# An uneven pace of expert dot products beside two delta-net layers, and a re-ordered opening of the first stretch, in a one-core decoder kernel on Trainium2

## What is computed

```
def peer_ffn(h, wq, k1, k2, u, v):
    ...
    v1, i1 = lax.top_k(s1, PEER_TOPK)
    v2, i2 = lax.top_k(s2, PEER_TOPK)
    ...
    sc, pos = lax.top_k(cand, PEER_TOPK)
    idx = jnp.take_along_axis(cand_idx, pos, axis=-1)
    gate = jax.nn.softmax(sc, axis=-1).astype(h.dtype)
    ...
        ue = jnp.take(u, ib, axis=0)
        act = gb * jax.nn.gelu(jnp.einsum('nd,nkd->nk', tb, ue))
        ve = jnp.take(v, ib, axis=0)
        return jnp.einsum('nk,nkd->nd', act, ve)
```

## Time and profile before

| | |
|---|---|
| median of three executions | 1930.27 us (1926.15 to 1933.41) |
| the profiled execution | 1927.03 us |
| its span, first to last instruction | 1925.2 us |
| instructions | 22276 |
| PE / DVE / ACT / POOL busy | 79% / 69% / 22% / 30% of the span |
| mean granted TensorE clock | 0.874 of full speed |
| read from HBM | 700.82 MB, 365 GB/s over the span |

### The profile page before, as it was taken

How to read it: one execution, slowest core, us unless ns; L and a number is a source line. 1 busy time by engine, 2 the same in 40 slices (tenths; PEclk the granted TensorE clock), 3 DMA queues, 4 the chain that set the end, 5 groups by cost and what they waited for, 6 DMA issues and landing times.

```text
span 1925.2 us, 22276 instructions
## 1 busy us (share of the span) xinstructions
PE 1529.6 (79%) x7828; PEld 912.6 (47%) x7828; DVE 1334.0 (69%) x3962; ACT 418.5 (22%) x1139; POOL 583.4 (30%) x551
## 2 busy tenths in 40 slices
PE   6999999965656889888889687998889875555555
PEld 6644876511113656666558265766656641111111
DVE  6667646769976779585446776877845579778654
ACT  1221211000002722622211264154121210000001
POOL 0110223444442322322222322232232244444541
PEclk8999798667678989999899898999998987886887
DMA  9988499999998967987999998699699999999995
GB/s 368 360 319 308 183 402 376 411 422 421 421 421 356 421 270 273 421 317 277 393 409 417 391 398 321 223 388 373 232 385 396 421 379 403 421 421 421 422 422 227
DMA packets 100255, 703.32 MB, mean 365 GB/s; under 512 B 15264, under 2 KB 15648, under 8 KB 16560
## 3 DMA queue, kind: packets, MB, share of 16 engines
q0 software_dynamic: 78336, 570.46, 73.6%
q1 hardware_dynamic: 21808, 131.45, 17.0%
HBM read 700.82 MB, written 1.05 MB: 365 GB/s over the span
## 4 chain that ended last, share of the span: by engine, by line
PE 43%; DMA 20%; DVE 15%; issue 5%; ACT 5%; POOL 1%; SPq 0%; DVEq 0%; POOLq 0%; ACTq 0%
PE PS L1646 15%; DMA vb<-in_peer_uv,idx 8%; DMA ub<-in_peer_uv,idx 6%; PE PS L1796 3%; PE PS L1702 3%; PE PS L2013 3%; PE PS L1989 3%; DMA ring<-in_peer_uv,idx 2%; DVE vb L1147 2%; PE PS L1970 2%; DVE ub L1147 2%; PE PS L1749 2%; PE PS L1873 1%; ACT ring L1472 1%; DMA mods<-in_peer_uv,idx 1%
## 5 line engine op out<-in xcount | busy, mean ns | idle before, releaser
L1646 PE MATMUL PS<-ub,z 128*64 128x512 f32 x832 | 342.7, 762 | 128.4 <-DVE z L1113 125.0
L1646 PE MATMUL PS<-vb,z 128*64 128x512 f32 x828 | 318.4, 748 | 106.9 <-DVE z L1113 105.2
L2046 POOL DMA_INDIRECT ub<-in_peer_uv,idx x208 | 227.4, 1093 | 522.4 <-PE PS L1646 458.2
L2046 POOL DMA_INDIRECT vb<-in_peer_uv,idx x207 | 230.8, 1115 | 434.9 <-PE PS L1646 389.2
L1359 ACT ACTIVATE tanhs<-cubed 128x2 f32<-128x2 f32 x256 | 52.0, 203 | 879.0 <-DVE cubed L1102 855.5
L1646 PEld LDWEIGHTS PS<-ub,z 128*64 128x64 f32 x832 | 77.8, 162 | 279.0 <-DVE z L1113 184.4
L1646 PEld LDWEIGHTS PS<-vb,z 128*64 128x64 f32 x828 | 73.7, 160 | 262.9 <-DVE z L1113 170.4
L1147 DVE CUSTOM_DVE_ANT_0 vb<-vb,h 128x1024 f32<-128x1024 f32 x104 | 127.1, 1222 | 54.0 <-DMA vb<-in_peer_uv,idx 53.4
L1646 PE MATMUL PS<-mods,z 128*64 128x512 f32 x204 | 124.8, 743 | 36.9 <-DVE z L1113 34.5
L1147 DVE CUSTOM_DVE_ANT_0 ub<-ub,h 128x1024 f32<-128x1024 f32 x104 | 127.1, 1222 | 35.7 <-DMA ub<-in_peer_uv,idx 33.6
L1106 DVE SCALAR_TENSOR_TENSOR acts<-tanhs,gated_x 128x2 f32<-128x2 f32 x256 | 40.4, 158 | 152.4 <-ACT tanhs L1359 146.1
(11 more groups left out here) (364 smaller groups left out, 2780.2 us busy)
## 6 DMA issues: line engine op xcount, KB each, us to landing
ring<-in_gdn_qkv SPq DMA_DIRECT2D x32, 1024.0 KB
ring<-in_peer_wq SPq DMA_DIRECT2D x23, 1024.0 KB
two_slots<-in_ada_wide POOLq DMA_DIRECT2D x20, 1024.0 KB, 7.8
ring<-in_gdn_z SPq DMA_DIRECT2D x16, 1024.0 KB
ring<-in_gdn_w_out SPq DMA_DIRECT2D x16, 1024.0 KB
ring<-in_gla_w_in SPq DMA_DIRECT2D x6, 2048.0 KB, 11.0
mods<-in_ada_wide POOLq DMA_DIRECT2D x11, 1024.0 KB, 7.5
ring<-in_ada_w SPq DMA_DIRECT2D x4, 2048.0 KB, 11.9
```

What stands on the lines that cost most here:

```text
L1646: last = pe.matmul(y[64 * g:64 * g + 64, e, :], z[:, i % 4, g, :], rows[:, D + e * 512:D + (e + 1) * 512], start=False, stop=False, skip_g ...
L2046: pool.indirect_dma_start(row_buffers[b], None, uv_rows, off).then_inc(row_landed[b].sem, 16)
```

## The change

One kernel takes these changes together:

- `dot_at` for stretches 1 and 2 goes by a table `PACE` of (nominal time, dots done): 17 dots by 86, 45 by 164, 60 by 236, 88 by 314, 128 by 520. Routing stays at its dot numbers.
- `JOB_AT` spaces jobs 4 to 11 from 3.0 to 63.0 (from 2.5 to 39.5), and the eight "mod" blocks go from 52 + 8b to 85 + 27b; DVE's use of their sum moves to behind them.
- The first use of the row buffers goes in the order 0 to 3, 8, 9, 10, 4 to 7, so that the four in `vb` come last, and POOL waits for `cols_summed` ahead of dot 7; ahead of dots 4 and 5 it has waits of their own.
- On PE `turn_h` of tile 1 goes ahead of the 40 narrow matmuls.
- ACT's wait for the last state product of a core gets a due time of its own, later than it had.

```
-                return W_AT[w] + (W_AT[w + 1] - W_AT[w]) * (n + 1) / STRETCH
+            PACE = ((0.0, 0), (86.0, 17), (164.0, 45), (236.0, 60), (314.0, 88), (B, STRETCH))
...
+                if w in (0, 3):
+                    return W_AT[w] + A * (n + 1) / STRETCH
+                (at, of), (to, upto) = next((a, b) for a, b in zip(PACE, PACE[1:]) if n + 1 <= b[1])
+                return W_AT[w] + at + (to - at) * (n + 1 - of) / (upto - of)
...
-            JOB_AT = (-31.0, -27.0, -15.0, -11.0, 2.5, 6.5, 10.5, 14.5, 18.5, 25.5, 32.5, 39.5)
+            JOB_AT = (-31.0, -27.0, -15.0, -11.0, 3.0, 10.5, 18.0, 25.5, 33.0, 43.0, 53.0, 63.0)
...
+            FIRST = (0, 1, 2, 3, 8, 9, 10, 4, 5, 6, 7)
...
-                    b = min(free, key=lambda i: (users[i][-1] if users[i] else -1, i))
+                    b = min(free, key=lambda i: (users[i][-1] if users[i] else FIRST.index(i) - len(FIRST)))
...
-                        yield 45 + 13.0 * 7
+                        yield 85 + 27.0 * 7 + 20
...
+                                yield core.at("U", 0) + core.dt * 14.5
                                 act.wait_ge(ds_done.sem, ds_count(t, hf, last_of(t), 1))
...
-                        pe.wait_ge(x_mixed.sem, 3)
+                        yield 1.0
+                        pe.wait_ge(h_ready.sem, h_ready.at(4))
+                        turn_h(pe, 1)
+                        pe.wait_ge(x_mixed.sem, 4)
                         pe.wait_ge(wide_used.sem, WIDE)
                         for m in range(COLUMNS):
-                            yield -5.0
+                            yield 1.5
...
-                            yield 52 + 8.0 * b
+                            yield 85 + 27.0 * b
...
                             if n == 4:
+                                pool.wait_ge(wide_used.sem, WIDE)
+                            if n == 5:
+                                pool.wait_ge(mixed.sem, 2 * T)
+                            if n == 7:
                                 pool.wait_ge(cols_summed.sem, 1)
```

3 lines of the change are left out of this document (removed).

## The result

The changed kernel takes 1962.6 us (median of four, 1956.3 to 1964.12) where the kernel before took 1931.3 beside it: a ratio of 1.0172, 95% interval 1.015 to 1.0194. It is 1.7% slower; the forecast was 1.0% faster. The profiled execution took 1956.3 us, its span is 1954.5.

A forecast was written before the change was run, and what follows sets the result against it. It took the cores to be bound by PE and DVE taking turns, not memory. Each stretch's -31 + 18 + 1.5 made -22.5 for both, the opening +3: 1927.0 became 1907.5, 1911 as a median; range 1877 to 1941.

The forecast's parts named there:

- The pace, where pairs go: Cores of stretches 1 and 2: nine added pairs at 2.0 us each cost 18 us a stretch.
- Which its gaps can mostly take: Solve levels in the cores: with more pairs DVE needs some 1.9 us more a level, mostly fitting its idle gaps.
- upper bound of a pair's price: Cores: 5.6 us a pair if PE's 1.94 and DVE's 3.7 both stood in the chain.
- rival C: Cores of stretches 1 and 2: DVE becomes their bound, 39 us more DVE work a stretch, slower at 1949; chance 0.16.
- The order of waits: Cores: main danger, a dot lacking rows or a free `z` slot stands ahead of a solve step; no size given.
- The pace, where pairs leave: Convolutions and tails of stretches 1 and 2: nine pairs fewer at 3.4 us each give back 31 us a stretch.
- rival B: Convolutions and tails: memory sets the pace, giving back 44 us a stretch; 1881, or down to 1863; chance 0.17.
- Routing: Cores of stretches 1 and 2: some 5.5 us more routing work on DVE each stretch, 1.5 us on the path.
- ACT's wait: Cores: the later wait for the last state product; nothing taken, bounds 0 and -8 us a stretch.
- The opening of stretch 0: Start of stretch 0: `turn_h` first makes memory rest 8 us instead of 3, spread jobs help; net +3 us.
- threshold of 3.3 us a pair: Cores: the price of a pair from which rival C, slower, decides.
- D: Stretches 1 and 2: pairs give back 1.94 us and cost 2.0, so work only moves; 1933; chance 0.25.

The follow-up runs named there:

- later pairs: The changed kernel with PE's part of a pair due two dots later in stretches 1 and 2: 1945.25 us, 1.0093 of the kernel before.
- both repairs: The changed kernel with PE's part of a pair two dots later and two routing calls moved out of the cores: 1939.64 us, 1.0062 of before.
- The shift by four: The kernel before with ACT's later wait and dots 8 to 95 of stretches 1 and 2 due 4.0 nominal us later: 1.001 of before.

## Why the prediction was wrong, step by step

**The pace, where pairs go.** This is the step that failed. It put a price of 2.0 us on a pair, "near PE's price", and multiplied by nine: 18 us, and 19.5 with routing. The cores grew by 40.9 and 40.5, 4.5 a pair, within the 0 to 5.6 that I had given. But the term is of the wrong kind, not only too small. Half of the shift costs 33 us, the reverse of it has longer cores with fewer pairs, and the even pace shifted by two makes the two stretches 27.2 and 19.7 us longer for no pair at all. One half of what was lost, 41 of 81 us, lies in the levels of the solve, where the place of dot and pair is shown to count; the 1.94 us of PE for each of the six pairs added there would make 11 of it. The row that I used myself says it: the level of 8.0 us with the pair at the same place at 708.23 and at 716.21. I read it as an engine that is just full. It was, but with nothing else in the chain only because two orders were in step. "Which its gaps can mostly take" holds for a gap at the right place only. The other half lies outside these levels, at 3.3 us a pair where I took 2.0; why is open. Followed back in the two profiles, the chain runs through the pairs' matmuls for 73 us of the four cores before and 102 after, through dots for 39 and 56, through routing for 7 and 20.

**A sum that counted routing twice.** DVE's 236.57 us of stretch 3 hold three routing calls, 46.6 us in L1012 to L1072. Dots and what belongs to a pair take 192 us, so 1.5 a dot and 3.0 a pair, not 3.7. The upper bound of a pair's price was thus 4.9 and not 5.6, and the DVE work of rival C 33 us a stretch and not 39. (The slices also reach 422 GB/s, not 421; nothing hangs on that.)

**The order of waits.** What the prediction named as its main danger is there: 57 us of waits for `z` against 27. It is a part: without these waits 15 of the 33 us come back, and the cores are still 33 and 21 us too long. Rows held a dot for 5.4 us, in the second core of stretch 1 alone, so that half of the sentence was borne out only in small. It comes up with the repairs: 21 us with later pairs, 26 with both. Some 60% of the busy time taken off either engine comes off the cores (38 of 61 us for dots, 25.6 of 40 for pairs), partly as shorter waits. Of the 18 to 31 us a stretch that remain with both repairs nearly all lie outside the levels (43 of 48 in the two stretches); how they divide between work, waits for rows and bad places no run tells.

**The pace, where pairs leave.** Forecast 31 us a stretch, measured 24.4 and 20.3: 2.7 and 2.3 a pair, between PE's 1.94 and the middle of 3.4 that I took. The first convolutions gave 4.3 each, the second ones 8.8 and 5.5, against 5 to 8 forecast; the tails 15.5 and 13.2, against 15 to 20; and the heads took back 4.2 and 2.7, which I had not looked at. The mechanism was right, the size 7 and 11 us a stretch too large. In the tail PE is still 89% and 97% busy in output projection and queries, and the memory went down to 379 and 368 GB/s there: no sign of it setting the pace alone. The two sums do not bear out the 4.9 a pair, memory's price, that rival B took where pairs leave.

**Routing.** Forecast 1.5 us a stretch, 0 to 5.5. Moved out of the cores it gives back 12 us of the two stretches, about 6 each. That is the whole of a call, and the forecast was for the 5.5 us of it that the pace had moved in, so it bounds the term from above and does not measure it. With the even pace it gives nothing.

**ACT's wait.** Nothing was taken for it. The shift by four has this edit too and is at 1.001 (0.9982 to 1.0039), so the two together cost nothing that can be measured.

**The opening of stretch 0.** Forecast +3, between -3 and +9; measured -4 by the ratio of 0.998 (0.996 to 1.0), -3.7 in the stretch's length: just outside. The first dot of stretch 1 came 6.4 us sooner than before's, outside the -3 to +9 named as a sign, but 2.7 of that lie ahead of the first dot of stretch 0, which stands anywhere from 221.8 to 230.8 in the runs. The chain was as described. The changed kernel's rows, in order of time on the three engines:

```profile
213.94 0.99 POOL L2059 DMA_INDIRECT ub<-in_peer_uv,idx  x1 [23.47 <-DVE idx L1080]
...
219.45 1.23 DVE L410 TENSOR_TENSOR h<-h,mods 128x1024 f32<-128x1024 f32 x1
...
220.82 1.94 PE L387 MATMUL PS<-ident,h 128*128 128x128 f32 x8 [7.64 <-DVE h L410]
222.56 17.06 PE L1737 MATMUL PS<-ones,vb 128*128 128x1 f32 x80
...
239.89 0.93 POOL L2059 DMA_INDIRECT vb<-in_peer_uv,idx  x1 [17.17 <-PE PS L1737]
```

PE idles 7.64 us for `h` (forecast 7 to 8), the narrow matmuls take 17.06 (16 to 17), `vb`'s gathers are issued 17.17 us behind POOL's last, and the memory all but rests from 234 to 240:

```profile
228.00:234.00 6.00, 6.00 (x30) 6.00 (x30) 2.94 (x8) 0.00 (x0) 0.00 (x0) 0.50 1.00 419
234.00:240.00 6.00, 6.00 (x29) 6.00 (x29) 0.00 (x0) 0.00 (x0) 0.11 (x1) 0.50 0.07 27
```

Buffers and `turn_h` cost 8 us where I had 5, the jobs' spread gave 8 where I had 2: the term that was mis-sized is the jobs. I had counted only the rest in one slice; as I read the windows, PE's jobs had kept pairs, and by them buffers, back over the whole of 216 to 300 (360 GB/s before, 382 with the jobs spread). On the clock: in the changed kernel it was granted at 0.50 from 216 to 240, from within the gap on. The version with the narrow matmuls first has no such gap: PE is busy for 5.97 of 6 us and more in its windows from 200 us on, with a clock of 1.00 up to 213, where the narrow matmuls begin. It then has 0.50 as well:

```profile
216.00:222.00 6.00, 6.00 (x30) 6.00 (x30) 3.29 (x8) 2.48 (x4) 4.78 (x5) 0.50 0.94 337
```

So 0.50 was granted here with a gap ahead and without one. What `turn_h` ahead costs is the wait and its place.

**The rivals.** C came nearest in time (1949 against 1962.6), its threshold of 3.3 us a pair was passed, and so was its sign of cores 15 us longer (15.9 to 24.6). But DVE is 70 to 83% busy in the cores, not over 92%, so it is not their bound; and without the routing counted twice C would have been at 1936. Its nearness is luck in that part. D and B are out by the cores. The range, 1877 to 1941, took in at its upper end only a part of rival C; the upper bound of 5.6 a pair that I had worked out myself, and a core that grows for another cause than its pairs, had no weight in it.

## What to carry to other kernels

Where two instruction orders are merged for engines that keep them, as PE did here (it idled 2.73 us for `z` with L1888 queued behind the pair), and both are periodic, look for a common period before changing the rate of either: write down both periods (here 8.07 and 8.13 nominal units), and see in the trace whether the beside-work starts at the same place in each turn of the chain. If it does, what it costs there (in the level shown, a pair's 1.94 us of PE and nothing for its dots) it costs at that place only (shifted by two, the levels shown took 10.7 and 12.3 us instead of 8.0), and no price per piece from such a row held here for another rate; the cheap test is to shift one order by a part of the period with the work unchanged. When such a change moves several parts at once, run the halves: here a gain of 16 us lay in one half with one of its edits undone.
